# Mixture-of-experts encoder layer: gate and up products with the weights stationary and the tokens moving

## What is computed

```python
cap = CAPACITY_FACTOR * N // N_EXPERTS          # 128 sample tokens, 64 prompt tokens
aff = jax.nn.softmax(hf @ w_router, axis=-1)
gates, idx = lax.top_k(aff.T, cap)
xe = hf[idx]                                    # (16, cap, 1024)
a = jnp.einsum('ecd,edf->ecf', xe, w_gate)      # w_gate, w_up: (16, 1024, 512)
u = jnp.einsum('ecd,edf->ecf', xe, w_up)
ye = jnp.einsum('ecf,efd->ecd', jax.nn.silu(a) * u, w_down)   # w_down: (16, 512, 1024)
out = jnp.zeros_like(hf).at[idx].add(gates[..., None] * ye)
```

## Time and profile before

| | |
|---|---|
| median of 3 runs | 1623.55 us (1623.14 to 1625.81) |
| the profiled execution, device time | 1623.36 us |
| its span, first to last instruction | 1621.5 us |
| mean granted TensorE clock | 0.947 of full speed |
| the stage of the experts on PE, first to last matmul | about 942.6 to 1437.8 us |
| PE busy over the span | 1447.0 us (89%) |

### The profile page before, as it was taken

The page is one execution under the profiler, slowest core; times in us unless marked ns, Lnnn a source line. Parts: engine busy times, 40 slices in busy tenths (PEclk is TensorE's granted clock), DMA queues, the critical chain, the costliest instruction groups (busy, mean ns, idle before and its releaser), DMA issues. The chain is left out here.

```text
span 1621.5 us, 21520 instructions
## 1 busy us (share of the span) xinstructions
PE 1447.0 (89%) x7320; PEld 1016.2 (63%) x7320; DVE 932.7 (58%) x1324; ACT 721.8 (45%) x1157; POOL 182.2 (11%) x255
## 2 busy tenths in 40 slices
PE   5999997599999969869998969999999999948997
PEld 4777775365565535458887746666666666627885
DVE  5444443377677748723347856677676676643553
ACT  4333433376666747722221544444444444423332
POOL 1111111000000000010000111112112121021110
PEclk9999998699999979989998979999999999978999
DMA  8533322713111054064432756878878788753331
GB/s 257 94 111 110 110 97 85 252 64 114 70 63 55 20 190 156 29 208 156 140 123 87 262 169 220 263 252 270 256 261 267 254 262 265 245 164 126 126 135 65
DMA packets 118847, 261.53 MB, mean 161 GB/s; under 512 B 7648, under 2 KB 37472, under 8 KB 115720
## 3 DMA queue, kind: packets, MB, share of 16 engines
q1 hardware_dynamic: 110592, 233.55, 41.2%
q0 software_dynamic: 7168, 25.17, 6.7%
q10 hardware_dynamic: 1032, 2.10, 1.1%
HBM read 194.20 MB, written 66.58 MB: 161 GB/s over the span
## 5 line engine op out<-in xcount | busy, mean ns | idle before, releaser
L1742 DVE TENSOR_TENSOR moe_w_lo<-ring,moe_w_hi 128x2048 fp32r<-128x2048 f32 x96 | 220.3, 2296 | 163.5 <-ACT moe_w_hi L1681 163.4
L1681 ACT ACTIVATE moe_w_hi<-ring 128x2048 fp32r<-128x2048 f32 x96 | 183.7, 1914 | 204.0 <-PE moe_p_g L1864 82.2
L1413 PE MATMUL mix_p_big<-kept_out_w,mix_m_hi 128*128 128x512 f32 x384 | 126.4, 411 | 4.6 <-DVE mix_m_lo L1288 2.4
L510 PE MATMUL proj_p_out<-proj_w_hi,proj_h_hi 128*128 128x512 f32 x264 | 110.8, 420 | 9.5 <-DVE proj_q_hl L408 9.5
L1872 PE MATMUL moe_p_gu<-ring,moe_xT_r 128*64 128x512 f32 x512 | 116.9, 598 | 0.0
L510 PE MATMUL proj_p_out<-proj_w_lo,proj_h_hi 128*128 128x512 f32 x264 | 105.0, 398 | 0.0
L510 PE MATMUL proj_p_out<-proj_w_hi,proj_h_lo 128*128 128x512 f32 x264 | 104.9, 397 | 0.0
L962 DVE TENSOR_REDUCE sample_ntop<-sample_p_s 128x1 f32<-128x1024 f32 x64 | 78.2, 1222 | 37.4 <-PE sample_p_s L784 36.7
L798 PEld LDWEIGHTS sample_p_t<-sample_ident_r,sample_probs_r 128*128 128x128 f32 x688 | 73.1, 142 | 23.2 <-ACT sample_probs L900 6.6
L1413 PEld LDWEIGHTS mix_p_big<-kept_out_w,mix_m_hi 128*128 128x128 f32 x384 | 73.1, 196 | 21.4 <-issue 2.6
L798 PE MATMUL sample_p_t<-sample_ident_r,sample_probs_r 128*128 128x128 f32 x688 | 80.1, 246 | 5.0 <-ACT sample_probs L900 2.5
(11 more groups left out here) (298 smaller groups left out, 3122.4 us busy)
## 6 DMA issues: line engine op xcount, KB each, us to landing
ring<-in_w_gate SPq DMA_DIRECT2D x32, 1024.0 KB, 5.6
ring<-in_w_up SPq DMA_DIRECT2D x32, 1024.0 KB, 7.6
ring<-in_w_down SPq DMA_DIRECT2D x32, 1024.0 KB, 7.2
qT_d<-proj_qT SPq DMA_DIRECT2D x12, 1024.0 KB, 3.9
sample_q<-qT_d SPq DMA_DIRECT2D x8, 1024.0 KB, 5.3
proj_x<-in_x SPq DMA_DIRECT2D x12, 512.0 KB, 4.3
proj_w_raw<-in_w_in SPq DMA_DIRECT2D x8, 768.0 KB, 5.6
kT_d<-proj_kT SPq DMA_DIRECT2D x12, 512.0 KB, 3.6
```

What stands on the lines that cost most here:

```text
L510: last = pe.matmul(p_out[:, cols], h[:, s, k, :], w[:, k, cols], start=(k == 0 and n == 0), stop=(k == KC - 1 and n == 2))
L1413: mm = pe.matmul(p_out[:, cols], m[:, s, k, :], ww[:, k, cols], start=(k == 0 and n == 0), stop=(k == KC - 1 and n == 2))
L1681: act.activation(w_hi[:, at % SPLIT], raw[:, at % RAW], ACT.Copy).then_inc(hi_made, 1)
L1742: dve.tensor_tensor(w_lo[:, at % SPLIT], raw[:, at % RAW], w_hi[:, at % SPLIT].bitcast(F32), ALU.subtract).then_inc(lo_made, 1)
```

## The change

In gate and up the operands change roles. The weights are stationary, a 128x128 block at a time, and the tokens move: the 128 sample rows and the 64 prompt rows side by side, 192 columns (ALL = S + R). So the prompt's gate and up are made of the same three fp32r products as the sample's, and xT_hi and xT_lo hold both. The output is [hidden, tokens], already as down needs it: turn_hidden goes away, SiLU and the multiply are one instruction each for all 192 columns, and ACT and DVE make hT_hi, hT_lo and hT_r straight from the SBUF tile hid. A unit of gate or up is now the whole contraction for 256 of the 512 hidden columns; the order of units is gate, gate, up, up, down, down. down keeps its form.

The host lays the weights out by unit, so that a partition's 8 KB of a unit lie together in HBM. With the raw gate and up no longer read by PE, their loads wait for lo_made, those of down for pair_done as before. p_g and p_u take two banks each, so p_t has one bank in place of two: x is turned in three rounds of one bank (4 blocks, 4 blocks, the prompt's 8 blocks), placed in PE's list ahead of down's first half, between its halves, and behind its second half (expert 0's rounds use the still free banks of p_y as well). The three functions called step in the diff are, in this order, those of ACT, DVE and PE. Gathers run two experts ahead in POOL's list in place of three.

```diff
 def expert_unit(w_gate, w_up, w_down, e, j):
-    w, row = ((w_gate, w_up)[j % 2], e) if j < 4 else (w_down, e - 1)
...
+    w, row = ((w_gate, w_up)[j // 2], e) if j < 4 else (w_down, e - 1)
+    w = w[row, j % 2] if isinstance(row, int) else w[bass.ds(row, 1), j % 2].rearrange("a p n -> (a p) n")
+    return w.rearrange("p (k c) -> p k c", c=BANK)
...
-                    sp.wait_ge(pair_done, (n - RAW) // 2 + 1 if is_int(n) else
-                               first_pair(e) + j // 2 - RAW // 2 + 1)
+                    if j < 4 or (is_int(e) and e == 1):
+                        sp.wait_ge(lo_made, n - RAW + 1)
+                    else:
+                        sp.wait_ge(pair_done, e - 1)
...
-                    pool.wait_ge(t_done, x_round(e - 1) + X_ROUNDS)
+                    pool.wait_ge(t_done, e * ROUNDS)
...
-            for e in range(3):
+            for e in range(2):
                 gather(e)
             for e in range(E):
-                if e + 3 < E:
-                    gather(e + 3)
+                if e + 2 < E:
+                    gather(e + 2)
                 scatter(e)
...
+            def silu_of(e):
+                act.wait_ge(unit_done, first_unit(e) + 2)
                 if later(e, 1):
+                    act.wait_ge(mul_made, e)
+                act.activation(by_bank(silu), hidden(p_g), ACT.Silu).then_inc(silu_made, 1)
+            def hidden_high(e):
+                act.wait_ge(mul_made, e + 1)
...
+                act.activation(hT_hi[:], hid[:, :, 0:S], ACT.Copy).then_inc(h_hi_made, 1)
...
             def step(e):
                 if inside(e):
                     split(e, 3)
                     split(e, 4)
+                    silu_of(e)
                     split(e, 5)
-                    silu_sample(e)
+                    if inside(e + 1):
+                        x_high(e + 1, 0)
                     split(e, 6)
-                    silu_prompt(e)
                     if inside(e + 1):
-                        x_high(e + 1)
+                        x_high(e + 1, 1)
                     if inside(e - 1):
                         split(e, 7)
+                    if inside(e + 1):
+                        x_high(e + 1, 2)
+                    if inside(e - 1):
                         split(e, 8)
                     hidden_high(e)
...
+            def x_low(e, r):
+                dve.wait_ge(x_hi_made, e * ROUNDS + r + 1)
+                dve.tensor_tensor(part(xT_lo, r), turned(e, r).rearrange("p (k c) -> p k c", c=S if r < 2 else R),
+                                  part(xT_hi, r).bitcast(F32), ALU.subtract).then_inc(t_out, 1)
...
             def step(e):
                 if inside(e):
                     for t in (3, 4, 5):
                         split(e, t)
-                    multiply_sample(e)
+                    multiply(e)
+                    if inside(e + 1):
+                        x_low(e + 1, 0)
                     split(e, 6)
-                    multiply_prompt(e)
-                    if inside(e + 1):
-                        x_low(e + 1)
...
                 if inside(e - 1):
+                    weigh(e - 1, 0)
+                if inside(e + 1):
+                    x_low(e + 1, 1)
+                if inside(e - 1):
                     if inside(e):
                         split(e, 7)
-                    weigh(e - 1, 0)
-                    if inside(e + 1):
-                        x_prompt(e + 1)
+                    weigh(e - 1, 1)
+                if inside(e + 1):
+                    x_low(e + 1, 2)
+                if inside(e - 1):
                     if inside(e):
                         split(e, 8)
-                    weigh(e - 1, 1)
                     weigh(e - 1, 2)
                     weigh(e - 1, 3)
                 if inside(e):
                     hidden_low(e)
...
+            def inner(out, at):
+                hi, lo = (w[:, at % SPLIT].rearrange("p k c -> p (k c)").rearrange("p (k c) -> p k c", k=KC)
+                          for w in (w_hi, w_lo))
+                for c in range(2):
+                    block = slice(c * P, (c + 1) * P)
+                    for k in range(KC):
+                        for n, (w, x) in enumerate(((hi, xT_hi), (hi, xT_lo), (lo, xT_hi))):
+                            mm = pe.matmul(out[:, c * ALL:(c + 1) * ALL], w[:, k, block], x[:, k, :],
+                                           start=(k == 0 and n == 0), stop=(k == KC - 1 and n == 2))
+                mm.then_inc(unit_done, 1)
...
+            def gate_up(e):
+                pe.wait_ge(t_out, e * ROUNDS + ROUNDS)
+                for j, n, at in units(e)[:4]:
+                    pe.wait_ge(lo_made, n + 1)
+                    if j % 2 == 0 and later(e, 1):
+                        pe.wait_ge((silu_made, mul_made)[j // 2], e)
+                    inner((p_g, p_u)[j // 2][:, j % 2, :], at)
...
             def step(e):
                 if inside(e):
-                    gate_up(e, 0)
-                    gate_up(e, 1)
-                    if inside(e + 1):
-                        turn_x(e + 1)
...
+                    gate_up(e)
+                if inside(e + 1):
+                    turn_x(e + 1, 0)
                 if inside(e - 1):
-                    down(e - 1)
-                if inside(e):
-                    turn_hidden(e)
+                    down_half(e - 1, 0)
+                if inside(e + 1):
+                    turn_x(e + 1, 1)
+                if inside(e - 1):
+                    down_half(e - 1, 1)
+                if inside(e + 1):
+                    turn_x(e + 1, 2)
+                if inside(e - 1):
+                    down_prompt(e - 1)
```

More of the change, by code:

```diff
@@ L1723, in _ @@
             split(0, 1)
-            x_high(0)
+            for r in range(ROUNDS):
+                x_high(0, r)
             split(0, 2)
@@ L1814, in _ @@
             split(0, 1)
-            x_low(0)
-            x_prompt(0)
+            for r in range(ROUNDS):
+                x_low(0, r)
             split(0, 2)
@@ L1859, in sample @@
-            def sample(out, at, x_hi, x_lo, k0, start, stop):
+                        mm = pe.transpose(out[:, b * S:(b + 1) * S], xs_r[:, k * P:(k + 1) * P], ident_r[:])
+                    else:
+                        mm = pe.transpose(out[:, b * R:(b + 1) * R], xr_r[:, b * P:(b + 1) * P], ident_r[0:R, 0:R])
+                mm.then_inc(t_done, 1)
+            def inner(out, at):
[8 more added lines that the diff above has]
+                mm.then_inc(unit_done, 1)
@@ L1861, in sample @@
+            def sample(out, at, x_hi, x_lo):
                 for k in range(FC):
@@ L1863, in sample, with prompt @@
                     for n, (x, w) in enumerate(((x_hi, hi), (x_hi, lo), (x_lo, hi))):
[L1864 to L1865 removed]
+                        mm = pe.matmul(out, x[:, k, :], w, start=(k == 0 and n == 0), stop=(k == FC - 1 and n == 2))
                 mm.then_inc(unit_done, 1)
[L1868 removed]
+            def prompt(out, at, x):
@@ L1870, in prompt @@
                 for k in range(FC):
                     for half in range(2):
-                        mm = pe.matmul(out[half * R:(half + 1) * R, :], x[:, k0 + k, :], raw[:, (at + half) % RAW, k, :],
-                                       start=(start and k == 0), stop=(stop and k == FC - 1))
+                        mm = pe.matmul(out[half * R:(half + 1) * R, :], x[:, k, :], raw[:, (at + half) % RAW, k, :],
+                                       start=(k == 0), stop=(k == FC - 1))
                 mm.then_inc(pair_done, 1)
-            def gate_up(e, half):
-                if half == 0:
-                    pe.wait_ge(t_out, x_round(e) + X_ROUNDS)
-                for j, n, at in units(e)[2 * half:2 * half + 2]:
+            def gate_up(e):
+                pe.wait_ge(t_out, e * ROUNDS + ROUNDS)
+                for j, n, at in units(e)[:4]:
@@ L1880, in gate_up @@
                     pe.wait_ge(lo_made, n + 1)
-                    if half == 0 and later(e, 1):
-                        pe.wait_ge((silu_made, mul_made)[j], e * 2 - 1)
-                    sample((p_g, p_u)[j % 2][:], at, xT_hi, xT_lo, half * FC, half == 0, half == 1)
-                if half == 0 and later(e, 1):
-                    pe.wait_ge(mul_made, e * 2)
-                prompt(p_gu, at - 1, xT_r, half * FC, half == 0, half == 1)
-            def down(e):
-                pe.wait_ge(t_out, h_round(e) + H_ROUNDS)
-                for j, n, at in units(e + 1)[-2:]:
-                    pe.wait_ge(lo_made, n + 1)
-                    if later(e, 1):
-                        pe.wait_ge(weighed, e * 4 - 3 + (j - 4))
-                    sample(p_y[:, j - 4, :], at, hT_hi, hT_lo, 0, True, True)
-                if inside(e + 2):
-                    turn_x_prompt(e + 2)
+                    if j % 2 == 0 and later(e, 1):
+                        pe.wait_ge((silu_made, mul_made)[j // 2], e)
@@ new lines, in gate_up, with down_half, down_prompt @@
```

(16 more changed lines are left out.)

140 lines of the change are left out of this document (50 added, 90 removed).

## The result

The changed kernel takes **1683.62 us** (median of 4 runs, 1681.1 to 1686.1) against 1624.68 for the kernel before in the same session: ratio 1.0358, 95% interval 1.0341 to 1.0375. It is slower, as forecast, and within the stated range (up to 1690), but by 59 us where +29 was forecast: the difference is twice what I said. The profiled execution took 1683.03 us with a span of 1681.2.

The account below looks back on a forecast made before the run. PE was taken to bound the experts' stage. About +2.0 us a step gave +30.7 us over the steps; with ends of -1.6, about +29 on 1623.4 made 1652 us, range 1632 to 1690.

Parts of the forecast that it names:

- some 230: PE's matmuls: below some 230 moving columns the load of the stationary block sets the pace.
- The first rival: Gate and up: loads hidden behind the columns, about 0.089 us a matmul, kernel faster at about 1598 us; chance 0.12.
- The second rival: Gate and up: narrow fp32r matmuls at float32's pace, about 2350 us, or the clock falls to its lower level; together 0.07.
- The step on the wait for x_low 1: Third turning round (round 2): PE waits for DVE's x_low 1 because p_t has one bank, +0.5 us a step.
- the price of a matmul: Gate and up: 0.107 us per 192-column matmul, 192 of them 20.5 us, +2.1 us a step.
- The turning rounds: Turning x on PE: two rounds of 4 blocks at 0.47 us and one of 8 at 0.77, +0.2 us a step.
- the ends: Start and last step of the experts' stage: +2.2, -0.5 and -3.3 us, together about -1.6 us.
- down as now: Weight loads on SP's queue: down's are issued as before the change, costed at nothing.
- not read before down in the next step, 20 us later: hT_hi, hT_lo and hT_r made from SBUF: costed at nothing, since down reads them only 20 us later.
- now hid is ready long before: -3.3: Last step: PE's 1.8 us wait for hT_r and 1.5 us of lower-clock matmuls go away, -3.3 us.
- The start gains about 0.5: Start of the experts' stage: expert 0's turning rounds have banks of their own, a gain of about 0.5 us.
- the +2.2: Step 0, with no down between the turning rounds: 5.7 us before becomes some 8, +2.2 us.

Follow-up runs that it names:

- e1: Changed kernel with the loads of the last expert's down waiting for lo_made in place of pair_done 15; 1670.0 us.
- e2: Changed kernel with the experts' first two loads (up of expert 1) also waiting until expert 0's prompt-row gather has landed; 1680.38 us.

## Why the prediction was right or wrong

**Right: the bound and the mechanism.** PE bounds the stage before and after; in the steady part it is busy 99%. That the load sets the pace for few columns is shown by the runs with 64, 128 and 256 columns, though not the figure "some 230" at which it stops. The first rival (loads hidden, 1598 us) would have needed 0.089, and 0.1117 was measured. Its price was taken from transposes, and their loads are shorter: 0.14 us where those of gate and up have 0.19, four of them in 0.40:

```profile
1202.30 0.40 PEld L1833 LDWEIGHTS moe_p_t<-moe_ident_r,ring_r 128*128 128x128 f32 x4
```

The second rival's first half (float32's pace) did not come. Of its other half, the lower clock, there was a little at expert 1, behind the pauses of the turning: the clock was 0.50 from 978 to 988 us, the first 4 us of gate_up in it. The kernel before has the same, for less time (step 1 took 1.3 us more than its later steps, and takes 1.8 more after the change). From there to the last step the clock stayed up:

```profile
978.00:988.00 10.00, 5.25 (x28) 4.95 (x28) 4.39 (x5) 2.12 (x4) 2.15 (x2) 0.50 0.64 227
```

The step on the wait for x_low 1 was right in place and a little large: PE stands 0.36 us there, counted between starts (0.5 said, the releaser named as said). From expert 2 on gate_up was never held up by x_low 2, nor a turning round by a gather, although the gather's median landing went from 5.0 us to 11.3 under the burst of loads: the cover was enough.

**A term mis-sized: the price of a matmul.** "I take 0.107, nearest to the two load rows": it is 0.1117. The rows of before had it. The earlier trace rows has 15 loads, between which there are 14 distances and not 15: (1.75 - 0.19) / 14 = 0.111, where I had 0.104. With the earlier trace rows's 0.11 both rows give the price that was measured. The slip in the price costs 192 x 0.0047 = 0.9 us a step. The turning rounds (0.31, 0.30 and 0.73 us, where 0.47, 0.47 and 0.77 were said) and the shorter wait gave 0.5 of it back: a step is +2.4, not +2.0. Over 14 steps, with the clock at expert 1, this is the 33.9 against 28.0 of the table.

**The step that failed: the ends, "together about -1.6".** They were +19.4 in the first and last stretch where -2.5 was dealt to them. This is 22 of the 30 us by which the forecast was short, and two things carry it. One is in what I costed at nothing: "gate and up may start earlier than now, down as now; at a step's start up to five are queued", with the cover counted from a step's start, that is, under gate_up. "down as now" was not true of the last step: its loads were issued 18 us ahead of the end of the prompt's down of expert 14 before, and right behind it now. And I did not ask what covers them in the one step without a gate_up. Run e1 priced that: 13.6 us. The same step lacks the cover of hT_hi and hT_lo, "not read before down in the next step, 20 us later". So "now hid is ready long before: -3.3" failed as well: hid is ready, but hT_lo stands last in DVE's list, and even with the loads early PE stands for 2.4 us where it stood for 1.8 before. The other is the start: "The start gains about 0.5" looked at PSUM banks and not at the queue. The earlier loads met the gather, +4.3, of which e2's trace gave back 3.9.

**Expert 0's stretch.** Of its +6.2, +3.3 lie in gate_up (24.4 us against 21.2, both with their first 6 us at the lower clock) and +2.9 in the turning behind it (8.5 against 5.6). Forecast were +2.1 and +1.5. In the second is a slip of the sum: the 5.7 us of before hold the turning of the hidden rows, so the -0.9 and +0.2 of that step were counted on top of the +2.2.

The sum: 13.6 + 3.2 from the two ends, about 34 from 14 steps and 6 from expert 0 make 57 of the 59 us.

## What to carry to other kernels

Before making the weights stationary, compare the moving columns with what a load of the stationary block costs: here a matmul with a 128x128 block of fp32r weights cost 0.112 us however few columns moved, so with 192 columns part of each load's time went unused. One load for 384 columns gave back 3.5 us a step (28.96 in place of 32.5). A cover that holds in the loop must be looked for again in the first and in the last step, where the work that covers isn't there. And a load that may start earlier is a change of its own: ask what shares the queue with it then.

## What the hardware showed that was not expected

The clock. In the kernel with 128 columns in the corrections it was at 1.2 GHz from the start of expert 0's gate_up (950.1) to 1045.4, 95 us, although PE had work without a pause while gate and up ran. It rose 4 us after matmuls of 512 columns had begun (1041.4); in the kernel with 64 columns it rose 3 us after (1045.6, 1048.3). With 192 columns throughout it rose 4 to 7 us into gate_up in the traces of four kernels. So leaving columns out cost 34 and 37 us in one run each. Why it stays down is not settled by these rows; it is only seen that the kernels differ in the columns they move.

The load of the stationary block also isn't one price: eight transposes of fp32r data took 0.71 us here, 0.089 each, with 128x128 blocks as well, while the fp32r matmuls of gate and up never came closer than 0.111 on average, even with 64 moving columns in two of three.
